# Experts with few tokens: ScalarE splits the next weight piece ahead of its wait for the joined gate rows

## The reference, cut to what matters

```python
def swiglu(h, w_gate, w_up, w_down):
    return (jax.nn.silu(h @ w_gate) * (h @ w_up)) @ w_down

def moe_swiglu(h, w_router, b_router, w_gate, w_up, w_down):
    ...
    top_logits, top_idx = lax.top_k(logits, TOP_K)
    ...
    for e in range(N_EXPERTS):
        y_e = swiglu(h, w_gate[e], w_up[e], w_down[e]).astype(F32)
        out = out + gates[..., e:e + 1] * y_e
```

## Time and profile before

| | us |
|---|---|
| median of 3 runs | 2826.08 (2826.08 to 2830.97) |
| the profiled execution | 2825.76 |
| its span, first to last instruction | 2824.1 |
| turns 22 to 27, join to start of turn 28 | 1526.53 to 1641.00 |
| turns 28 to 34 (pairs), about | 1641 to 1830 |

### The profile page before, as it was taken

One profiled execution on the slowest core, in us unless ns is written; L12 is line 12 of the kernel. 1 busy time (PEld: TensorE's weight loads), 2 busy tenths in 40 slices (PEclk: granted clock), 3 DMA queues, 4 the chain that ended last, 5 costly groups with the idle time before them and its releaser, 6 DMA issues.

```text
span 2824.1 us, 43102 instructions
## 1 busy us (share of the span) xinstructions
PE 2673.2 (95%) x18156; PEld 2377.1 (84%) x18156; DVE 1921.0 (68%) x2040; ACT 1477.4 (52%) x1687; POOL 116.2 (4%) x112
## 2 busy tenths in 40 slices
PE   7778999998998999999998899999999999999998
PEld 5667999988897887888886678888888899999998
DVE  7885656656745445875447876588888678766877
ACT  5314554456643334664336655467777565446543
POOL 7251000000000000000000000000000000000000
PEclk9899999999998999999999999999999999999999
DMA  5102545543424545885546875589999535534553
GB/s 206 61 2 92 163 155 189 194 150 105 149 75 171 191 174 196 302 321 195 180 176 255 332 278 211 214 304 351 353 342 362 205 130 182 188 116 143 193 181 120
DMA packets 219856, 558.31 MB, mean 198 GB/s; under 512 B 8592, under 2 KB 167440, under 8 KB 176400
## 3 DMA queue, kind: packets, MB, share of 16 engines
q1 hardware_dynamic: 217584, 553.47, 55.2%
q10 hardware_dynamic: 2080, 2.10, 0.2%
HBM read 554.48 MB, written 1.05 MB: 197 GB/s over the span
## 4 chain that ended last, share of the span: by engine, by line
PE 80%; DVE 9%; ACT 4%; issue 2%; DVEq 2%; DMA 1%; POOL 0%; POOLq 0%; ACTq 0%; SPq 0%
PE ps L886 23%; PE ps L888 23%; PE ps L887 22%; DVE w_lo L3508 2%; DVE w_lo L1853 2%; PE ps L1701 1%; PE ps L1702 1%; DVE more_lo L3508 1%; PE ps L1678 1%; ACT arena L1822 1%; DVEq L2608 1%; PE ps L1721 1%; ACT w_hi L1837 1%; PE ps L924 1%; PE ps L1129 1%
## 5 line engine op out<-in xcount | busy, mean ns | idle before, releaser
L1853 DVE TENSOR_TENSOR w_lo<-ring,w_hi 128x1024 fp32r<-128x1024 f32 x362 | 447.4, 1252 | 254.2 <-ACT w_hi L1837 248.2
L1837 ACT ACTIVATE w_hi<-ring 128x1024 fp32r<-128x1024 f32 x362 | 379.8, 1058 | 371.8 <-PE ps L888 356.2
L3508 DVE TENSOR_TENSOR w_lo<-ring,w_hi 128x2048 fp32r<-128x2048 f32 x168 | 384.0, 2289 | 173.7 <-ACT w_hi L1825 173.4
L886 PE MATMUL ps<-x_hi,w_hi 128*128 128x256 f32 x1600 | 459.3, 287 | 16.0 <-DVE w_lo L1853 7.9
L887 PE MATMUL ps<-x_lo,w_hi 128*128 128x256 f32 x1600 | 453.6, 284 | 0.0
L888 PE MATMUL ps<-x_hi,w_lo 128*128 128x256 f32 x1600 | 453.6, 283 | 0.0
L1825 ACT ACTIVATE w_hi<-ring 128x2048 fp32r<-128x2048 f32 x168 | 321.4, 1915 | 210.2 <-PE ps L888 135.8
L886 PEld LDWEIGHTS ps<-x_hi,w_hi 128*128 128x128 f32 x1600 | 308.0, 193 | 22.3 <-issue 16.3
L887 PEld LDWEIGHTS ps<-x_lo,w_hi 128*128 128x128 f32 x1600 | 308.3, 193 | 0.4
L888 PEld LDWEIGHTS ps<-x_hi,w_lo 128*128 128x128 f32 x1600 | 308.0, 192 | 0.0
L3508 DVE TENSOR_TENSOR more_lo<-ring,more_hi 128x2048 fp32r<-128x2048 f32 x84 | 192.4, 2290 | 87.6 <-ACT more_hi L1825 86.8
(11 more groups left out here) (451 smaller groups left out, 5832.4 us busy)
## 6 DMA issues: line engine op xcount, KB each, us to landing
ring<-moe SPq DMA_DIRECT2D x252, 1024.0 KB, 5.6
more_raw<-moe SPq DMA_DIRECT2D x84, 1024.0 KB, 5.2
ring<-ffn_w_up SPq DMA_DIRECT2D x44, 1024.0 KB, 5.1
ring<-ffn_w_down SPq DMA_DIRECT2D x22, 1024.0 KB, 4.8
ring<-xa_w_kv SPq DMA_DIRECT2D x16, 1024.0 KB, 5.3
ring<-w_in SPq DMA_DIRECT2D x16, 1024.0 KB, 5.5
ring<-da_w_qkv SPq DMA_DIRECT2D x12, 1024.0 KB, 5.1
ring<-ff_w_gate SPq DMA_DIRECT2D x11, 1024.0 KB, 5.4
```

The source lines that it names most:

```text
L886: mm(o, lhs[0], rhs[0], start=start, stop=False)
L1837: nc.scalar.activation(w_hi[:, half_slot(at, half), :], ring[:, s_, half * 1024:half * 1024 + 1024], ACT.Copy).then_inc(hi_ready, 1)
L1853: nc.vector.tensor_tensor(w_lo[:, i, :], ring[:, s_, half * 1024:half * 1024 + 1024], w_hi[:, i, :], ALU.subtract).then_inc(lo_ready, 1)
L3508: nc.vector.tensor_tensor(lo, raw_piece(n), hi, SUB).then_inc(piece_lo, 1)
```

## The change

In the 14 turns whose last unit is packed, `high(n + 5)` is called inside `gate_to_silu`, between the copy of the low rows and the wait for the join, and no longer behind the silu. All other turns keep their order (and turn 0 has no such piece).

```diff
-            def gate_to_silu(g):
+            def gate_to_silu(g, between):
...
                     if is_packed(u):
                         act.wait_ge(turned, w - 1)
                         copy(prod[0:64, w % 2, :], ps[64:128, gate_bank(w), :]).then_inc(low_rows_out, 1)
+                        between()
                         act.wait_ge(gate_joined, packed_before(w) + 1)
                         src = silu[:, w % 2, :]
...
-                gate_to_silu(g)
-                if g:
+                behind = is_packed(units_of(g)[-1])
+                gate_to_silu(g, lambda: high(n + 5))
+                if g and not behind:
                     high(n + 5)
                 n = first_piece(g + 1)
```

## The result

The changed kernel takes 2821.34 us, the median of 20 runs (2815.14 to 2824.26), against 2828.26 us of the kernel before in as many (2825.42 to 2833.55). The ratio is 0.9974, with a 95% interval from 0.9968 to 0.9981: 0.26% or 7 us faster, where 11.1 us were forecast. The forecast time was 2815.0; of the 6.3 us between it and 2821.34, 2.2 come from the kernel before, whose median of 20 runs lies higher than that of the 3 runs I started from. The time is inside the range given, 2811.5 to 2822, close to its upper end.

What follows compares the result with a forecast made beforehand. TensorE, busy 95% of 2824.1 us, bounds the kernel. Six turns, each the longer of old length less 2.21 and 17.1 us, go from 114.47 to 103.4: 11.1 us saved, 2814.7, forecast 2815.0 us, range 2811.5 to 2822.

Steps and rivals of the forecast that it cites:

- The place: Join of turn 22 to start of turn 28, 114.47 us: all savings lie there; turn 21 and pair turns cost 0.
- The step of 2.21 us: In each of six turns from join 22, the second subtraction starts earlier, shortening the turn by 2.21 us, not 2.50.
- the floor from transfers: In the six turns, a piece takes 2.85 us to transfer, so no turn is shorter than 17.1 us.
- The forecast's own range: For the whole kernel, 2813.2 to 2816.5 us, from a piece in 2.75 to 2.90 us; forecast's chance 0.62.
- (1): Six turns: transfers hold only their long-stretch 352 GB/s, 17.87 us a turn; saving 7.2 us, total 2818.9; chance 0.18.
- (2): Six turns: idle time returns as waits for arrivals; 18.29 us a turn, saving 4.7 us, total 2821.4; chance 0.12.
- The signs: If right: 2.50 us waits gone in turns 22 to 27, six turns about 103 us, transfer share over 0.95.
- the sign of rivals (1) and (2): ScalarE's waits for `ring<-moe` and `more_raw<-moe` grow by over 10 us.
- The sign for failure as a whole: The moved split waits for its piece until after the join, or TensorE shows new idle time in turns 28 to 34.
- the memory side of about 358 GB/s: Weighed rule on HBM loads: a turn takes at least 17.6 us, saving 9 us; chance counted in (1).
- (3): Six turns: no floor from transfers; 13.9 us saved, total 2812.2 us; chance 0.04.
- (4): Pair turns: silu behind a split awaiting a late piece holds up TensorE; slower by over 0.2%; chance 0.04.

Runs made afterwards that it cites:

- halved transfers: Changed kernel with transfers of pieces 130 to 165 cut to half their columns: ratio 0.9959 to the kernel before, stage 101.66 us.
- short splits: Changed kernel with split and subtraction of pieces 130 to 165 on 256 of 2048 columns: ratio 0.9926 to the kernel before, stage 97.4 us.

## Why the prediction came out as it did

**The place was right.** The stage before turn 28 is where TensorE starves. With the split moved there alone the whole gain appears, with it moved in the pair turns alone nothing does, and those turns kept their 150.3 us. The silu of the packed unit in turn 29 starts 1.67 us after the start of the join where it was 0.71: about 1 us later, as foreseen, and it costs nothing.

**The step of 2.21 us was right.** The subtraction starts with the join's end, the next one waits 0.30 us behind the silu's split, and in turns where pieces are in time a turn is shorter by about this (turn 22 took 17.13 us in the first execution and 17.09 in the second, where it had taken 19.27). With halved transfers the turns took 17.08, 18.03, 15.89, 17.07 and 16.54 us; old lengths less 2.21, and less the 0.67 of the third, are 17.06, 17.86, 15.94, 17.07 and 16.52. Only the sixth turn didn't follow: up to TensorE's start of turn 28 it took 17.01 us (1613.70 to 1630.71), where 18.30 less 2.21 is 16.09.

**The term that was mis-sized is the floor from transfers, "17.1 us a turn".** From the kernel before I took a rate for it, 2.85 us a piece, as if the transfers were a pipe that is merely 0.88 full. The runs show that a pipe was not the limit: with buffers released early it carries a piece in 2.5 us (a turn in 15.1). Dividing a rate by its share, which gave the 374 GB/s behind this term, doesn't find that limit: it gives 373 for the changed kernel as well, and 413 with short splits. What sets the floor is the trip of a buffer. From the issue, a piece took 7.3 us to land, 1.9 for the split and 2.3 for the subtraction, 11.5 us together; over four buffers 2.9 us a piece or 17.3 us a turn at the least, and the buffers' waits in the two engines' orders come on top, for 18.2 us a turn in the first execution. In the second, with a landing of 6.9 us, the sum is 16.7 and a turn took 17.5. Before, with a landing of 5.7 us, the same sum gives 9.9 us or 14.9 us a turn, well under the 19 that a turn took; a floor that looks so far off comes nearer when the turns get shorter, as the landing grows with the overlap. So the saving up to TensorE's start of turn 28 was 6.2 and 9.0 us in the two profiled executions of the changed kernel, not 11.1, which agrees with the 7 us of the medians. The term of 17.1 us lies close to the least that the trip allows (16.7 to 17.3), but that is luck, since it was got from a rate that doesn't bind.

**The range held, the forecast didn't.** The forecast's own range, with a saving of 9.6 to 12.9 us, doesn't reach the 7 us measured. The time lies in the range given because that was drawn past rivals (1) and (2).

**The signs.** The 2.50 us waits are gone, and in the second execution the stage ran at a share of 0.96; but it took 105 to 109 us and not 103. ScalarE's waits for pieces grew by 10.5 us in the first execution, the sign of rivals (1) and (2), and by 6.2 in the second. The sign for failure as a whole, a moved split that waits for its piece until after the join, came up in turns 26 and 27 of the first execution (1600.36 against the join's 1600.09, 1619.19 against 1618.89), and the change still gained. It was set too strictly.

**Rivals.** (2) named the mechanism: "each transfer is issued and needed sooner, and the idle time comes back as waits for arrivals, deeper than a mean rate shows". I had given it 0.12 and a saving of 4.7 us; it is the mechanism that acted, at a price between the forecast and its own. I argued against it that the share was 0.88 and that only one turn showed a late piece, which says how much slack there was at the old pace and nothing about the new one. (1), 7.2 us, has the right number, with a cause (a rate held over long stretches) that the 417 GB/s refute. By the same figure the memory side of about 358 GB/s, of "Where 436 GB/s comes from" in the Trainium skill's "DMA: Bandwidth & Descriptors", did not bind this core; the section gets it as half of a stack's 716 GB/s. The 407 to 435 GB/s of the slices lie near the 435 which the same section gives as the ceiling of the path into SBUF. (3), 13.9 us with no floor from transfers, is nearly what the stage gave with halved transfers: 13.8 us from join to join (115.42 - 101.66), and 12.8 up to TensorE's start of turn 28, as the prediction counts. (4) didn't occur.

**What stays open.** Why one execution of the changed kernel has pieces landing after 7.3 us and a stage of 109.25 us, and the next one, after 6.9 us, 105.25. A trip that binds passes each delay of a transfer on to the next, so small differences can add up; but that is argued, not shown.

## What to carry to other kernels

When a wait is taken away in front of a ring of buffers, work out the round trip of one buffer (landing at the new overlap, plus each step that holds it) and divide by the number of buffers. The quotient is a lower bound: what a buffer waits in the orders of the engines comes on top, here 0.1 to 0.4 us a piece. A mean transfer rate with a share under 1 says nothing on it: it can be far under what the transfers can do, and still be the most that the ring lets through. And the landing time itself grows with the number of transfers that overlap, here from 5.7 to 7.3 us, so the slack seen before a change is larger than the slack that is left.

## What the runs showed of the hardware

One core's transfers of 1 MiB pieces from HBM ran at 421 GB/s over 58 us, with at most four under way (3.5 on the average, from 8.9 us over 2.55 us a piece) and landing after 8.9 us (the median). ScalarE 78% and VectorE 95% busy did not keep them from 369 GB/s. The landing of a piece grew with the overlap. In the kernel before, a piece that was issued with nothing else under way landed after 4.7 us; the median was 5.7 us there at 329 GB/s, 7.3 us in the changed kernel at 347 GB/s, and 8.9 us with short splits at 417 GB/s. In the changed kernel ScalarE waited for pieces 23 times, in a stage in which the transfers ran well under what they can do.
